# Second block: short-convolution gate tiles inside the attention, low-rank gate columns with the values

## The reference, cut to what matters

```python
u = modulate(rmsnorm_2(x, ...), sh1, sc1) @ w_in[layer]     # and the same for the context tokens
# columns of w_in: gla q 192, k 192, v 384, low-rank gates 16 + 16, r 384,
#                  short conv b 256, c 256, x 256, attention q 384, k 384, v 384
g_f = log_sigmoid(glr_f @ wg2_fw + bg_fw) / 16              # g_b alike: gates of the gated linear attention
sc  = b_gate * dwconv3(c_gate * xh, w, bias)                # short convolution, 256 wide
na  = softmax(q k^T + bias) v                               # six heads, 64 wide
x   = x + g1 * (concat[gla, sc, na] @ w_out[layer])
x   = x + g2 * conv_ffn(...)                                # the feed-forward part follows
```

## Time and profile before

| | us |
|---|---|
| median of 3 runs (1432.37 to 1436.32) | 1433.04 |
| the profiled execution | 1431.62 |
| its span, first to last instruction | 1429.8 |
| second block, layer 0: first values and projection | about 381 to 543 |
| its gated attention | 543 to 565.5 |
| its attention | 565.5 to 616.2 |
| its output projection | 616.2 to 655.3 |
| layer 1: first values and projection | about 1027 to 1157 |
| its attention | 1173 to 1205.4 |

### The profile page before, as it was taken

One profiled execution on the slowest core, in us unless ns is written; L12 is line 12 of the kernel. 1 busy time (PEld: TensorE's weight loads), 2 busy tenths in 40 slices (PEclk: granted clock), 3 DMA queues, 4 the chain that ended last, 5 costly groups with the idle time before them and its releaser, 6 DMA issues.

```text
span 1429.8 us, 21911 instructions
## 1 busy us (share of the span) xinstructions
PE 1374.2 (96%) x8517; PEld 1182.9 (83%) x8517; DVE 1036.1 (72%) x1953; ACT 709.5 (50%) x1198; POOL 48.0 (3%) x67
## 2 busy tenths in 40 slices
PE   6999999999999999899999999999999988999997
PEld 5778987779978787577888888888988867899997
DVE  5697686978679885747798999666544756788854
ACT  6537666366644642734444443322345636666643
POOL 1000000000010012000000000000000210000000
PEclk9999999999999999998999999999999999999999
DMA  7643556335376521031455444577433321455553
GB/s 266 221 154 114 175 175 226 121 102 183 127 264 218 169 98 59 16 113 50 136 165 170 149 162 162 187 255 252 145 116 105 117 89 60 138 192 188 174 190 109
DMA packets 61943, 218.52 MB, mean 153 GB/s; under 512 B 7024, under 2 KB 9072, under 8 KB 61456
## 3 DMA queue, kind: packets, MB, share of 16 engines
q1 hardware_dynamic: 59200, 205.55, 43.2%
q0 software_dynamic: 2496, 11.56, 2.3%
q10 hardware_dynamic: 144, 0.00, 0.0%
HBM read 216.04 MB, written 1.05 MB: 152 GB/s over the span
## 4 chain that ended last, share of the span: by engine, by line
PE 77%; DVE 9%; ACT 8%; issue 3%; DMA 2%; DVEq 0%; SPq 0%; ACTq 0%
PE bank L584 18%; PE bank L586 18%; PE bank L585 18%; PE bank L600 5%; DVE DP L2122 3%; ACT WHI L1455 2%; DMA RAWB<-in_ws 2%; DVE WLO L2027 2%; PE bank L1271 1%; ACT L1455 1%; ACT NHI L1455 1%; PE bank L1404 1%; PE bank L645 1%; PE bank L873 1%; PE bank L1413 1%
## 5 line engine op out<-in xcount | busy, mean ns | idle before, releaser
L584 PE MATMUL bank<-NHI,WHI 128*128 128x256 f32 (+1 forms) x1392 | 463.4, 333 | 9.7 <-DVE WLO L2027 8.0
L2027 DVE TENSOR_TENSOR WLO<-RAWB,WHI 128x1024 fp32r<-128x1024 f32 (+1 forms) x276 | 328.3, 1192 | 179.0 <-ACT WHI L1455 178.2
L585 PE MATMUL bank<-NLO,WHI 128*128 128x256 f32 (+1 forms) x1392 | 457.5, 329 | 0.0
L586 PE MATMUL bank<-NHI,WLO 128*128 128x256 f32 (+1 forms) x1392 | 457.5, 329 | 0.0
L1455 ACT ACTIVATE WHI<-RAWB 128x1024 fp32r<-128x1024 f32 (+1 forms) x276 | 283.3, 1029 | 191.3 <-PE bank L586 103.8
L584 PEld LDWEIGHTS bank<-NHI,WHI 128*128 128x128 f32 x1392 | 264.3, 190 | 44.1 <-issue 11.0
L585 PEld LDWEIGHTS bank<-NLO,WHI 128*128 128x128 f32 x1392 | 264.5, 190 | 24.7 <-issue 1.4
L586 PEld LDWEIGHTS bank<-NHI,WLO 128*128 128x128 f32 x1392 | 264.4, 190 | 23.5
L2122 DVE CUSTOM_DVE_ANT_0 DP<-RAWB,CREP,PRM 128x1024 f32<-128x1024 f32 x120 | 153.9, 1282 | 7.9 <-DMA RAWB<-in_ws 2.5
L1455 ACT ACTIVATE CF<-bank,PRM 128x512 f32<-128x512 f32 (+1 forms) x88 | 59.2, 673 | 177.2 <-PE bank L586 175.0
L584 PE MATMUL bank<-HHI,WHI 128*128 128x256 f32 (+1 forms) x330 | 109.4, 331 | 0.2 <-DVE WLO L2027 0.2
(11 more groups left out here) (352 smaller groups left out, 1951.9 us busy)
## 6 DMA issues: line engine op xcount, KB each, us to landing
RAWB<-in_ws SPq DMA_DIRECT2D x364, 512.0 KB, 3.3
RAWB<-in_ws SPq DMA_DIRECT2D x32, 384.0 KB, 3.7
NB<-in_nab POOLq DMA_DIRECT2D x12, 256.0 KB, 3.2
CREP<-in_crep POOLq DMA_DIRECT2D x2, 1024.0 KB, 6.7
K<-in_c POOLq DMA_DIRECT2D x2, 896.0 KB, 5.7
K<-in_c POOLq DMA_DIRECT2D x1, 1344.0 KB, 8.6
X<-in_xt SPq DMA_DIRECT2D x4, 256.0 KB, 4.8
X<-in_xt POOLq DMA_DIRECT2D x1, 1024.0 KB, 6.9
```

Of the source, the lines that this page charges most:

```text
L584: nc.tensor.matmul(o, hi[:, w], xh, start=(i == 0), stop=False)
L585: nc.tensor.matmul(o, hi[:, w], xl, start=False, stop=False)
L586: ins = nc.tensor.matmul(o, lo[:, w], xh, start=False, stop=(i == slabs - 1))
L2027: V.tensor_tensor(WLO[:, k % SPL, 0:w], RAWB[:, u % RAW, 0:w], WHI[:, k % SPL, 0:w].bitcast(F32), ALU.subtract).then_inc(S("lo_ready"), 1)
```

## The change

- Tile `glr` is dropped. The 32 gate columns stand right behind the gated values in `w_in`, so the first value units become 416 wide (`VGW`) instead of 384. ACT copies the 32 extra columns of each token bank into `VG` (in `AM`, preset to 1.0 by POOL), PE transposes them after tile 0 (`turn_gates`, four transposes into bank 5), and ACT copies them into a tile `GLR` (`copy_gates`).
- `gates` runs after tile 1, all four at once; Abs follows there, Exp after tile 2, Ln after the first unit of the attention values, DVE's combination at the second unit, `sums` after tile 3. The rotations move to the third unit of the attention values, `rope` on DVE to the fourth. `NFIRST` is 3.
- `gqa` joins `LAT_ONLY`: in layer 1 it is computed over 256 tokens.
- The two `scb` tiles leave the projection. Their 16 slabs are multiplied in bank 3 inside the attention, at steps 0, 1, 2, 4, 5, 6 (layer 0: 3, 3, 2, 3, 3, 2 slabs) or 0 to 3 (layer 1: 4 each). They aren't copied to `ZB`: DVE's `short_gate` multiplies from the bank, at steps 3 and 7 or at step 4, and `short_conv` no longer has that multiplication.
- The output projection's first slabs move to steps 11 to 14 (layer 0) and 7 and 8 (layer 1). The high and low parts of the short-convolution and gated outputs move to steps 8 to 10 (layer 0) and 4 and 5 (layer 1). Two unit splits (`rest`) on ACT and DVE come into the attention.
- `rows` and `columns` use bank 3 instead of 7, after tiles 0 and 1, and 2. DVE's `modulation(3)` comes in the first unit of the attention values, behind that unit's `rest()`.
- 12 dot units instead of 20 run beside the projection, 8 beside the output tiles (`DOTS_OUT`). The second copy of the condition vectors (`CREP2`) is loaded in the attention, and its Silu is taken at the first output tile.

```diff
-LAT_ONLY = ("nq", "r", "scb", "scc", "scx")
+LAT_ONLY = ("gqa", "nq", "r", "scb", "scc", "scx")
+VGW = VW + 32
+SCB_AT = ({0: (0, 1, 2), 1: (3, 4, 5), 2: (6, 7), 4: (8, 9, 10), 5: (11, 12, 13), 6: (14, 15)},
+          {0: (0, 1, 2, 3), 1: (4, 5, 6, 7), 2: (8, 9, 10, 11), 3: (12, 13, 14, 15)})
+SCB_REST_AT, SCB_READ_AT = ((3, 7), (2, 4)), ({3: (0,), 7: (1,)}, {4: (0, 1)})
+SC_HI_AT, SC_LO_AT, GLA_HI_AT, GLA_LO_AT = (8, 4), (9, 5), (9, 4), (10, 5)
-DOTS_PROJ = (1, 1, 1, 2, 2, 1, 2, 2, 2, 2, 2, 2)
+DOTS_PROJ = (0, 1, 1, 1, 1, 2, 2, 2, 2)
+DOTS_OUT = (0, 2, 2, 1, 1, 2, 0, 0)
...
+                def turn_gates():
+                    pe.wait_ge(S("gl_ready"), me.nth("gl_ready", 4))
+                    if 5 in held:
+                        pe.wait_ge(*held[5])
+                    for t in range(4):
+                        ins = nc.tensor.transpose(bank[5][0:64, t * P:(t + 1) * P], VG[:, t].rearrange("p d k -> p (d k)"), cst("ident"))
+                    ins.then_inc(S("gl_turned"), 1)
...
-                        rows(7, 4 * h, 4 * h + 4)
-                    if l == 0 and i == NFIRST - 1:
-                        columns(7)
+                        rows(3, 4 * h, 4 * h + 4)
+                    if i == 0:
+                        turn_gates()
+                    if i == 1:
+                        pe.wait_ge(S("ld_c2"), 16 * 2 * (l + 1))
+                        pe.wait_ge(S("gl_ready"), me.nth("gl_ready"))
+                        for k in range(4):
+                            gates(k)
+                    if l == 0 and i == 2:
+                        columns(3)
+                    if i == 3:
                         sums()
...
+                def scb_slabs(i):
+                    for j in SCB_AT[l].get(i, ()):
+                        k, s = j // KS, j % KS
+                        if s == 0:
+                            if uc or k == 0:
+                                pe.wait_ge(*held[3])
+                            scb_unit[:] = [unit()]
+                        (hi, lo), (xh, xl) = scb_unit[0], rhs(s)
+                        w, o = slice(s * P, (s + 1) * P), bank[3][:, 0:TC] if uc else bank[3][:, k * T:(k + 1) * T]
+                        nc.tensor.matmul(o, hi[:, w], xh, start=(s == 0), stop=False)
+                        nc.tensor.matmul(o, hi[:, w], xl, start=False, stop=False)
+                        ins = nc.tensor.matmul(o, lo[:, w], xh, start=False, stop=(s == KS - 1))
...
                 for i in range(NFIRST):
                     rest()
                     dots_beside(i)
-                if l == 0:
-                    modulation(7)
                 for u in range(4):
                     rest()
-                    dots_beside(NFIRST + u)
+                    if l == 0 and u == 0:
+                        modulation(3)
                     if u == 1:
...
+                def short_gate(k):
+                    x = ZB[:, Z2["scx"] + k, 0:n]
+                    g = bank[3][:, 0:TC] if uc else bank[3][:, k * T:(k + 1) * T]
+                    V.tensor_tensor(x, x, g, ALU.mult).then_inc(S("sc_ready"), 1)
```

More of the change, by code:

```diff
@@ L76 @@
 CAP = float(np.float32(np.exp(80.0)))
-TILES2 = ["gqa", "gka", "gqk", "glr"] + ["scb"] * 2 + ["scc"] * 2 + ["scx"] * 2 + ["r"] * 3 + \
+SLOTS2 = ["gqa", "gka", "gqk"] + ["scb"] * 2 + ["scc"] * 2 + ["scx"] * 2 + ["r"] * 3 + \
     ["nk"] * 3 + ["nq"] * 3
-Z2 = {n: TILES2.index(n) for n in TILES2}
+Z2 = {n: SLOTS2.index(n) for n in SLOTS2}
+TILES2 = [n for n in SLOTS2 if n != "scb"]
 NZ2 = len(TILES2)
-NFIRST = 4
-LAT_ONLY = ("nq", "r", "scb", "scc", "scx")
+SLOT2 = [i for i, n in enumerate(SLOTS2) if n != "scb"]
+NFIRST = 3
+LAT_ONLY = ("gqa", "nq", "r", "scb", "scc", "scx")
 VW = 384
+VGW = VW + 32
 def param_columns():
@@ L147, in stream @@
     for l in range(DEPTH):
-        add([2 * VW] * 4)
+        add([2 * VGW] * 4)
         for i in range(NFIRST):
@@ L155, in stream @@
             dots(DOTS_PROJ[NFIRST + j] if l == 0 and NFIRST + j < len(DOTS_PROJ) else 0)
-        add([UNIT] * KS)
+        add([UNIT] * 2)
+        for m in range(KS):
+            add([UNIT])
+            dots(DOTS_OUT[m] if l == 0 else 0)
         for m in range(2 * FT):
@@ L514, in _ @@
                 for pr in range(NAH // 2):
+                    if l == 0 and pr == 2:
+                        pool.wait_ge(S("gpv_done"), 3)
+                        pool.dma_start(CREP2[:], crep).then_inc(S("ld_crep"), 16)
                     if pr >= 2:
@@ L1559, in residual @@
                         load_root_table()
+                    if m == 0 and after_first is not None:
+                        after_first()
                     if m >= KS:
@@ L1842, in tile @@
                     w = T if name in LAT_ONLY and not uc else TC
-                    z, g = ZB[:, i, 0:w], bank[me.next_tile()][:, 0:w]
-                    if name == "glr":
-                        ins = A(z, g, ACT.Identity, bias=cst("glrone"))
-                    elif name == "gqa":
+                    z, g = ZB[:, SLOT2[i], 0:w], bank[me.next_tile()][:, 0:w]
+                    if name == "gqa":
                         ins = A(z, g, scale=GDK ** -0.5)
@@ L2799, in end_of_gated @@
                             output_norm(k)
-                    if i == 3:
+                    if i in SCB_REST_AT[l]:
+                        rest()
+                    if i in SCB_READ_AT[l]:
+                        dve.wait_ge(S("unit_done"), me.u)
+                        for k in SCB_READ_AT[l][i]:
+                            short_gate(k)
+                    if i == SC_LO_AT[l]:
                         for k in range(2):
@@ L2916, in columns2 @@
             out.append(np.concatenate([q + P + np.arange(64), k + P + np.arange(64)]))
-        elif name == "glr":
-            out.append(np.concatenate([lf + np.arange(16), pad, lb + np.arange(16), np.full(80, -1)]))
-        else:
-            out.append(base[name] + (t - Z2[name]) * P + np.arange(P))
-    return out, v, nv
+        else:
+            out.append(base[name] + (t - TILES2.index(name)) * P + np.arange(P))
+    return out, [sb_ + k * P + np.arange(P) for k in range(2)], v, nv
 def constants():
@@ L3043 @@
         put(tm_units(w[:, nv:nv + VW]))
-        for c in cols2[NFIRST:]:
+        for c in cols2[NFIRST:] + scb:
             put(fm_units(w, c))
```

183 lines of the change are left out of this document (95 added, 88 removed).

## The result

The changed kernel takes 1426.12 us (median of 5 runs, 1425.21 to 1429.39) against 1434.88 us for the kernel before in the same comparison (5 runs, 1432.37 to 1436.32): a ratio of 0.995, with a 95% interval of 0.9935 to 0.9964. It is faster, and the time lies in the range of 1411 to 1428, but 12.7 us were forecast and by the ratio the gain is 7.2 us (5.2 to 9.3).

A forecast was written before the change was run, and what follows sets the result against it. TensorE, busy 96% of the span, was taken as the bound, idle mainly in the two attentions. The terms summed to -12.7 us from the profiled 1431.62, giving 1418.9, or 1420 as a median of runs; range 1411 to 1428.

The forecast's parts named there:

- Parts 1 to 5: Both projections: `glr` out -10.9, wider values +2.6, copies +0.9, gate turning +1.4, `gqa` over 256 tokens -2.6, waits -1.7 us.
- Part 2's extra copies: Four more small ACT copies per layer, hidden in layer 0, delaying layer 1's first tile: +0.9 us.
- Part 6: Layer 0's attention values: PE waits for DVE's modulation to free bank 3, +3.0 us, ends 0 and 4.
- Rival C: The modulation wait takes the granted clock down, 5 us at half speed costing 2.5: 1423 us, chance 0.12.
- Part 7: `scb` tiles moved from projections into attentions, 3.6 and 3.2 us hidden in idle time: -5.4 us, bounds -10.8 and +1.4.
- rival A: Attentions swallow nearly all the moved work, and denser work may keep the clock up: 1414 us, chance 0.17.
- Rival B: Attentions hide nothing: slabs delay the ring, waits reappear behind moved copies at steps 8 to 10: +6.8, 1427 us, chance 0.16.
- Part 8: Eight dot units, 20.5 us of DVE, moved to output tiles with 20.6 us free: cost 0, without cover up to 20.5.
- Rival D: Dots exposed among the output tiles if raw units arrive late, the norm waiting: slower, all exposed 1441 us, chance 0.05.

The follow-up runs named there:

- e5: The changed kernel with the two gate tiles back in the projection and the copies and first output slabs at their earlier steps: 1430.0 us, ratio 0.9962.
- e3: The changed kernel with only the weight splits of the two gate units moved to other steps in the attentions: 1423.2 us, ratio 0.9918.
- e4: The changed kernel with only layer 1's context copies moved, high parts one step later, low parts behind the last step: 1429.3 us, ratio 0.9954.
- e7: e3 with the context's copies spread over the steps and layer 0's first output slabs from step 12: 1416.0 us, ratio 0.9889.
- b1: e7 with the modulation read ahead of the low part and one dot unit back in the projection: 1410.4 us, ratio 0.9848.
- e8: e5 with the gated chain's steps two later, the modulation read first and one dot unit back in the projection: 1417.3 us, ratio 0.989.
- e1: The changed kernel with layer 0's modulation read from bank 3 ahead of the third value unit's low part: 1422.8 us, ratio 0.992.

## Why the prediction was right and wrong

- **Parts 1 to 5**, the tiles, values, gates: right in kind. Layer 1 gave 15.1 us for 14.5. Layer 0 gave 13.2 for 12.9, although its clock drop behind the modulation took 3.4 away, so the rest was 3.7 better than summed. Counted in the timelines, the 16 gate matmuls in one row take 1.67 us where three groups took 2.75 (saved 1.1), the four value units without them between 16.95 (the clock drop taken off) and not 17.87 (0.9; from start to start it is 0.6), the row units 2.56 for 3.31 (0.75), and a wait of 0.76 for a low part (at 498.67 us) is gone. For the first two the prediction had "0.3 together", for the others no term. That fewer changes of kind are the reason is not shown by a run of its own.
- **Part 2's extra copies**: +0.9 was too much. Layer 1's first tile waits 1.10 us for the last value copy, as in the earlier trace rows.
- **Part 6**: right, 2.89 us for 3.0. Its chain was followed instruction by instruction on each engine, and each link came out. The Trainium skill (ScalarE: Activation LUTs, "What ACT_TABLE_LOAD costs") adds a drain to the load; by it the wait would have been 4.4. The rows disagree with it here: the load starts at 421.21, right behind the tile's copy, and Exp at 422.50.
- **Rival C**, the clock: it did happen in the profiled execution, and cost 3.4 us and not 2.5. It got a chance of 0.12, which was low: with this wait the clock fell in three of seven profiles.
- **Part 7**: the step that failed. The 5.4 us became nothing that the runs can tell (e5). The step is the 3.6 and 3.2 us of slab time that were to hide in PE's idle time: in the changed kernel PE idles 7.1 and 5.7 us where it idled 6.5 and 5.8, so on balance nothing was hidden. The prediction counted PE's slabs against PE's idle time; it said of the copies that they "make new waits there" and of the weight splits that they "come in at steps 3 and 7", and gave neither a chain. The trace has a chain for each: an item of ACT between Exp and the copy of the probabilities, and, unnamed in the prediction, an item of DVE that waits for ACT ahead of the scaling. It said of the new wait on DVE that the scores ahead of it come later anyway. The wait that mattered was not the one for the gate tile but the one for the weight's high part just ahead of it. e3, e4 and e7 took these apart. With both out of the way (b1 against e8) 1.2 and 2.4 us are hidden, still not 3.6 and 3.2; why not more in layer 0 stays open. That the growth (7.5 and 1.7) meets the forecast (8.1 and 3.1) all the same is partly luck: 3.0 and 2.2 us of it are a clock that stayed up, which the prediction had under rival A.
- **Rival B**, nothing hidden, 1427: in this part what happened, growths of 13.2 and 6.6 against 11.7 and 6.3, and half by its mechanism: waits behind the moved copies, and behind the weight splits, which it doesn't name. It was weighed at 0.16 and the forecast at 0.45, though the prediction had the list of items put into the ring.
- **Part 8**: wrong by 3.4 us. "It fits, barely" compared sums (20.5 in 20.6 us). Of DVE's idle time 1.13 and 2.17 us lie ahead of the first dot, and time that has passed can't be filled, so DVE's last update ended 3.7 us behind the last tile. The second of them has the Silu that the same change put ahead of a weight copy, a chain that the prediction didn't follow. Rival D was the right mechanism at a smaller size and with another reason: among the output tiles DVE doesn't stand waiting for a raw unit, it simply had too much left.
- The four misses, 3.4 (clock), 5.1 and 3.5 (attentions) and 3.4 (dots), make 15.4. Against them stand 3.7, 0.6 and 1.5 us in and ahead of the projections, and the 3.3 us by which the start came out earlier than summed. Of these 1.7 are a clock drop (at 200 us) that the kernel before's profile has and the changed one's hasn't, and the rest is within the scatter: e1, e3, e4, e5 and e7, which differ from the changed kernel only behind that point, reach it at 398.5 to 400.8 us. The gated stage (-1.6) and the stretch to the end (+2.5) are mostly clock drops too, and these two are left as they are.

## What to carry to other kernels

Where engines hand items around in a ring, cost each thing that is put in by its place in every engine's order: what it waits for, and what stands behind it. Here filling idle time of PE gained nothing at first, because the filler's weight split and the copies it displaced lay on the ring's other engines; spread to one an item, or put where that engine has no ring work left, they cost less, 0.9 and 2.4 us less of PE's idle time. When two attentions are compared, compare PE's busy and idle time and not only the length: the granted clock moved the length by up to 3.4 us with the same waits. And when work is moved under a cover, add up the free time from where the work can first start, not over the whole stretch, and look at what its loads do where it is moved to.
